# Gates of two branches by Strassen's seven products in a one-core fp32 layer pair

## The reference, cut to what matters

```python
h = rms_norm_2(x, norm_g)
proj = h @ w_in
...
ys = jnp.stack([y_a, y_b, y_c, y_d], axis=0)
branch_d = jnp.einsum('nbsw,nwd->bsnd', ys, w_branch)
g = jax.nn.sigmoid(gates.reshape(bsz, s, N_BRANCH, d))
merged = jnp.sum(g * branch_d, axis=2)
return x + merged @ w_out
```

## Time and profile before

| | us |
|---|---|
| median of 3 runs | 1284.22 (1284.12 to 1284.44) |
| the profiled execution | 1284.06 |
| its span | 1282.3 |
| PE busy in the span | 1274.5 (99%) |
| DVE busy | 718.6 (56%) |
| ACT busy | 567.7 (44%) |
| POOL busy | 32.9 (3%) |

### The profile page before, as it was taken

The page is one execution under the profiler, slowest core; times in us unless marked ns, Lnnn a source line. Parts: engine busy times, 40 slices in busy tenths (PEclk is TensorE's granted clock), DMA queues, the critical chain, the costliest instruction groups (busy, mean ns, idle before and its releaser), DMA issues.

```text
span 1282.3 us, 16218 instructions
## 1 busy us (share of the span) xinstructions
PE 1274.5 (99%) x6041; PEld 1050.8 (82%) x6041; DVE 718.6 (56%) x1497; ACT 567.7 (44%) x1192; POOL 32.9 (3%) x71
## 2 busy tenths in 40 slices
PE   9999999999999999999999999999999999999998
PEld 8888777898888888888888888888878788888887
DVE  5367775754555545448574677764545524444454
ACT  5367665543453344334543323652344532322323
POOL 1000000100000000001100000000000000000000
PEclk9999999999999999999999999999999999999999
DMA  6243442126452646322522322122211222232231
GB/s 248 99 148 108 132 124 83 67 99 199 130 164 74 206 115 197 114 92 92 197 80 99 132 99 99 33 92 106 99 66 66 74 90 100 99 115 96 90 143 66
DMA packets 27038, 145.31 MB, mean 113 GB/s; under 512 B 3400, under 2 KB 3660, under 8 KB 12240
## 3 DMA queue, kind: packets, MB, share of 16 engines
q1 hardware_dynamic: 22920, 130.71, 28.8%
q0 software_dynamic: 1152, 8.39, 3.4%
q10 hardware_dynamic: 2888, 5.18, 1.3%
HBM read 135.87 MB, written 4.20 MB: 109 GB/s over the span
## 4 chain that ended last, share of the span: by engine, by line
PE 96%; DVE 1%; issue 1%; DMA 0%; ACT 0%; POOL 0%; SPq 0%; ACTq 0%; POOLq 0%; DVEq 0%
PE bank L1844 28%; PE bank L1846 27%; PE bank L1845 27%; PE sc L2012 3%; PE tp L2021 2%; PE ob L2078 1%; PE ob L2036 1%; PE bank L1946 1%; PE bank L1956 1%; PE bank L1963 1%; PE sc L1845 1%; PE sc L1846 1%; PE sc L1844 1%; DMA w_raw<-in_weights 0%; POOL rstd L593 0%
## 5 line engine op out<-in xcount | busy, mean ns | idle before, releaser
L1844 PE MATMUL bank<-xT_hi,w_hi 128*128 128x512 f32 (+1 forms) x1136 | 447.7, 394 | 0.1
L1846 PE MATMUL bank<-xT_hi,w_lo 128*128 128x512 f32 (+1 forms) x1136 | 436.4, 384 | 0.0
L1845 PE MATMUL bank<-xT_lo,w_hi 128*128 128x512 f32 (+1 forms) x1136 | 435.9, 384 | 0.0
L1152 DVE TENSOR_TENSOR w_lo<-w_raw,w_hi 128x512 fp32r<-128x512 f32 x412 | 262.4, 686 | 206.8 <-ACT w_hi L659 205.4
L659 ACT ACTIVATE w_hi<-w_raw 128x512 fp32r<-128x512 f32 x412 | 231.1, 621 | 83.6 <-PE bank L1846 80.4
L1844 PEld LDWEIGHTS bank<-xT_hi,w_hi 128*128 128x128 f32 x1136 | 213.7, 188 | 44.6 <-issue 4.5
L1846 PEld LDWEIGHTS bank<-xT_hi,w_lo 128*128 128x128 f32 x1136 | 213.4, 188 | 42.8
L1845 PEld LDWEIGHTS bank<-xT_lo,w_hi 128*128 128x128 f32 x1136 | 213.9, 188 | 39.8 <-issue 1.2
L667 ACT ACTIVATE arena<-bank 128x512 f32<-128x512 f32 x90 | 53.3, 597 | 200.7 <-PE bank L1846 195.6
L1844 PE MATMUL bank<-w_hi,act_hi 128*128 128x512 f32 (+1 forms) x264 | 102.7, 389 | 0.0
L1846 PE MATMUL bank<-w_hi,act_lo 128*128 128x512 f32 (+1 forms) x264 | 101.2, 383 | 0.0
(11 more groups left out here) (230 smaller groups left out, 1418.2 us busy)
## 6 DMA issues: line engine op xcount, KB each, us to landing
w_raw<-in_weights SPq DMA_DIRECT2D x101, 1024.0 KB, 4.8
arena<-in_weights POOLq DMA_DIRECT2D x8, 1024.0 KB, 9.5
arena<-in_weights SPq DMA_DIRECT2D x5, 1024.0 KB, 8.3
arena<-in_bias ACTq DMA_DIRECT2D x16, 256.0 KB, 2.9
act_lo<-act_lo SPq DMA_DIRECT2D x24, 128.0 KB, 2.8
x_sb<-in_x SPq DMA_DIRECT2D x4, 512.0 KB, 6.3
w_raw<-in_weights SPq DMA_DIRECT2D x4, 512.0 KB, 7.8
x_dram<-x_sb SPq DMA_DIRECT2D x1, 2048.0 KB, 11.8
```

What stands on the lines that cost most here:

```text
L1152: nc.vector.tensor_tensor(w_lo[SPLIT_AT[b]][:, cols], w_raw[SLOT[b]][:, cols], w_hi[SPLIT_AT[b]][:, cols].bitcast(F32), ALU.subtract).then ...
L1844: nc.tensor.matmul(ps, hi_l, hi_r, start=first, stop=False, skip_group_check=onto)
L1845: nc.tensor.matmul(ps, hi_l, lo_r, start=False, stop=False, skip_group_check=onto)
L1846: return nc.tensor.matmul(ps, lo_l, hi_r, start=False, stop=last, skip_group_check=onto)
```

## The change

The gates of "c" and "b" (`gate_quad`) are computed with h and the gate's weights cut in 2 x 2 blocks, features x tokens and features x features, by Strassen's seven products (Winograd's form). Each of the seven has 512 output features, 256 tokens and a depth of 512: in chunks, 2 halves x 2 chunks x 4 blocks x 3 products of 256 columns. Here output features lie on partitions.
- Weights: four blocks of 512 x 512 are loaded per branch, two of them a second time or into the extra places; G_SUM_1 to G_SUM_4 are made there by four accumulating transfers from POOL. Seven blocks are split instead of four. An accumulation for G_SUM_2 or G_SUM_4 waits for the split of the sum before it, since it adds onto the same place.
- x forms t1 to t4 (sums and differences of blocks of h, 128 x 1024 each) are made once and serve both branches. DVE makes a raw form from x_hi and x_lo, ACT rounds it, DVE subtracts for the low part. t1 is made in the gates of "d", behind DVE's `split(b + 1)` and ahead of the last four multiply-adds; t2, t3, t4 in "c", behind the splits of G_SUM_1, G_12 and G_SUM_2.
- Products go to `sc0/sc1`, `tp/ob` and `bank2/bank3` in pairs (`GATE_BANK`); ACT copies them out (the third, G_12, with the sigmoid), DVE adds them up in `sig_quad`, ACT applies the sigmoid to the three other quarters. `sig_quad` lies over the raw forms, so ACT waits for all four low parts before its first copy there.
- The multiply-adds then write over `sig_quad`.

The diff, cut to its core:

```diff
+GATE_QUADS = {"c": QUADS, "b": QUADS + 1}
+G_11, G_SUM_1, G_12, G_SUM_2, G_SUM_3, G_22, G_SUM_4 = range(7)
+GATE_BANK = (0, 2, 0, 1, 1, 1, 2)
+GATE_X = ("x11", "t1", "x21", "t2", "t3", "t4", "x22")
...
+        gate_bank = [[sc[0], sc[1]], [tp, ob], [bank[2], bank[3]]]
...
+            def load_gate_quad(f):
+                b = FIRST[f"quad{f}"]
+                load(b + G_11)
+                if f == QUADS:
+                    sp.wait_ge(pv_done, N_UNITS)
+                else:
+                    sp.wait_ge(w_split, PARTS * (FIRST[f"quad{f - 1}"] + G_SUM_4 + 1))
+                sp.dma_start(w_raw[2], stream[STREAM_AT[b, "21"], :, :]).then_inc(w_loaded[2], 16)
+                sp.dma_start(w_raw[3], stream[STREAM_AT[b, "11"], :, :]).then_inc(w_loaded[3], 16)
+                load(b + G_12)
+                load(b + G_22)
...
+            for f in GATE_QUADS.values():   # on POOL
+                b = FIRST[f"quad{f}"]
+                pool.wait_ge(w_loaded[2], 16 * LOADS[b, "21"])
+                add_gate_weights(2, b + G_22, w_chained)
+                pool.wait_ge(w_loaded[3], 16 * LOADS[b, "11"])
+                add_gate_weights(3, (b, "21"), w_paired)
+                pool.wait_ge(w_chained, 16 * (3 * f + 1))
+                pool.wait_ge(w_split, PARTS * (b + G_SUM_1 + 1))
+                add_gate_weights(2, b + G_11, w_chained)
+                pool.wait_ge(w_chained, 16 * (3 * f + 2))
+                pool.wait_ge(w_split, PARTS * (b + G_SUM_2 + 1))
+                add_gate_weights(2, b + G_12, w_chained)
...
+                split(b + G_SUM_1)              # ACT's gate_quad
+                act.wait_ge(gate_add, KD * (r - 1))
+                if f == QUADS:
+                    round_form(1)
+                split(b + G_12)
+                copy_out(G_11, lambda h: p1_of_gate[:, h, :].rearrange("p (m s) -> p m s", s=ST))
+                if f == QUADS:
+                    round_form(2)
+                split(b + G_SUM_2)
+                copy_out(G_SUM_1, lambda h: p5_of_gate[:, h, :].rearrange("p (m s) -> p m s", s=ST))
+                if f == QUADS:
+                    round_form(3)
+                    act.wait_ge(form_split, len(FORMS))
+                split(b + G_SUM_3)
+                copy_out(G_12, quarter(0, 0))
+                copy_out(G_SUM_2, quarter(0, 1))
+                split(b + G_22)
+                copy_out(G_SUM_3, quarter(4, 1))
+                split(b + G_SUM_4)
+                copy_out(G_22, quarter(4, 0))
...
                     split(b + 1)                # DVE's gates
+                    if (br, half) == ("d", 1):
+                        form("t1")
+                        split_form("t1")
                     for c in range(4):
...
+                plus, minus = {"t1": ("x11", "x12"), "t2": ("t1", "x22"), "t3": ("x22", "x12"), "t4": ("t2", "x21")}[n]
+                if plus in form_raw:
+                    combine(form_raw[plus], x_part[minus][0], (ALU.mult, ALU.subtract))
+                else:
+                    combine(x_part[plus][0], x_part[minus][0], ALU.subtract)
+                    combine(raw, x_part[plus][1], ALU.add)
+                combine(raw, x_part[minus][1], ALU.subtract, True)
...
+                split(b + G_SUM_1)              # DVE's gate_quad
+                if f == QUADS:
+                    form("t2")
+                    split_form("t2")
+                split(b + G_12)
+                if f == QUADS:
+                    form("t3")
+                    split_form("t3")
+                split(b + G_SUM_2)
+                if f == QUADS:
+                    form("t4")
+                    split_form("t4")
+                split(b + G_SUM_3)
+                split(b + G_22)
+                fold(0, 1, p1_of_gate, G_11, G_SUM_2)
+                fold(4, 1, p1_of_gate, G_SUM_3)
+                split(b + G_SUM_4)
+                fold(4, 1, p5_of_gate, G_SUM_1)
+                fold(4, 0, p1_of_gate, G_22)
+                split(b + len(LHS))
...
+                for i, name in enumerate(GATE_X):   # PE's gate_quad
+                    where, o = GATE_BANK[i], b + i
+                    if name in FORMS:
+                        pe.wait_ge(form_split, FORMS.index(name) + 1)
+                    for h in range(2):
...
+                        pe.wait_ge(quad_free[where][h], quad_drained(f, i) - 1)
+                        for m in range(2):
+                            for k in range(KW):
+                                if h == 0 and m == 0:
+                                    pe.wait_ge(w_split, PARTS * o + k + 1)
+                                at = W * k + P * (2 * h + m)
+                                last = product(gate_bank[where][h][:, ST * m:ST * m + ST], w_hi[SPLIT_AT[o]][:, at:at + P], w_lo[SPLIT_AT[o]][:, at:at + P],
+                                               x_hi[name][:, k, :], x_lo[name][:, k, :], opens and m == 0 and k == 0, k == KW - 1, True)
```

More of the change, by code:

```diff
@@ L137, in plan @@
     for br in ORDER:
+        if br in GATE_QUADS:
+            f = GATE_QUADS[br]
+            first[f"quad{f}"] = n
+            done += [("quad_full", 2 * (len(LHS) * f + i + 1)) for i in range(len(LHS))]
+            n += len(LHS)
         for half in range(2):
-            add(f"gate_{br}{half}", 2, 4)
+            if br not in GATE_QUADS:
+                add(f"gate_{br}{half}", 2, 4)
             add(f"branch_{br}{half}", 1, 4)
@@ L157, in places @@
     quads = {FIRST[f"quad{f}"]: f for f in range(QUADS)}
+    gate_quads = {FIRST[f"quad{f}"]: f for f in GATE_QUADS.values()}
     def loaded(b, where, place=None):
@@ L173, in places @@
             slot[b + SUM_1], slot[b + SUM_2], slot[b + SUM_3], slot[b + SUM_4] = 2, 2, 3, 2
+            b += len(LHS)
+        elif b in gate_quads:
+            loaded(b + G_11, ordinary % RING)
+            loaded((b, "21"), 2)
+            loaded(b + G_12, (ordinary + 1) % RING)
+            loaded(b + G_22, ordinary % RING)
+            loaded((b, "11"), 3, at[b + G_11])
+            slot[b + G_SUM_1], slot[b + G_SUM_2], slot[b + G_SUM_3], slot[b + G_SUM_4] = 2, 2, 3, 2
+            ordinary += 3
             b += len(LHS)
@@ L428, in quad_drained @@
         def quad_drained(f, i):
-            where = QUAD_BANK[i]
-            return QUAD_BANK.count(where) * f + QUAD_BANK[:i + 1].count(where)
+            order = QUAD_BANK if f < QUADS else GATE_BANK
+            return QUAD_BANK.count(order[i]) * f + order[:i + 1].count(order[i])
         def lhs_at(f, pair_, name):
@@ L649, in split_parts @@
                         if b - FIRST[f"quad{f}"] == SUM_3:
+                            act.wait_ge(w_paired, 16 * (f + 1))
+                    for f in GATE_QUADS.values():
+                        if b - FIRST[f"quad{f}"] in (G_SUM_1, G_SUM_2, G_SUM_4):
+                            act.wait_ge(w_chained, 16 * (3 * f + 1 + (G_SUM_1, G_SUM_2, G_SUM_4).index(b - FIRST[f"quad{f}"])))
+                        if b - FIRST[f"quad{f}"] == G_SUM_3:
                             act.wait_ge(w_paired, 16 * (f + 1))
@@ L1109, in gates @@
                             nc.scalar.activation(mT_hi[:, j, :], merged[:, j, :], ACT.Copy).then_inc(merged_rounded, 1)
+                    if half == 0:
+                        split(b + len(LHS) + 2)
             dsa = attention(U_DSA, N_UNITS, dsa_out)
@@ L1771, in gates @@
                             nc.vector.tensor_tensor(merged[:, j, :], merged[:, j, :], tmp[:, c % 2, :], ALU.add).then_inc(gate_add, 1)
[L1772 to L1775, removed]
+            x_part = {f"x{k + 1}{t + 1}": [part[:, KW * k:KW * k + KW, ST * t:ST * t + ST].bitcast(F32) for part in (xT_hi, xT_lo)]
+                      for k in range(2) for t in range(2)}
@@ L1853, in open_bank @@
                         pe.wait_ge(quad_free[e % 4 // 2][e % 2], quad_drained(f, len(LHS) - 1 if e % 4 >= 2 else PLAIN_21))
+                for br, f in GATE_QUADS.items():
+                    if 0 <= e - USE[f"branch_{br}0"] < 4 and e % 4 >= 2:
+                        pe.wait_ge(quad_free[2][e % 2], quad_drained(f, G_SUM_4))
             def feature_chunk(b, e, c, kc, rhs_hi, rhs_lo, tok=slice(0, S), full=True, steps=None, at=(), arriving=False):
@@ L2278, in _ @@
             for br in ORDER:
-                gates(br)
+                if br in GATE_QUADS:
+                    gate_quad(br)
+                else:
+                    gates(br)
             def merged_ready(i, t, ks):
@@ L2364, in weight_stream @@
         n = BRANCH[br]
+        if br in GATE_QUADS:
+            for kh, fh in ((0, 0), (0, 1), (1, 0), (1, 1)):
+                at = col["gates"][0] + D * n + W * fh
+                blocks.append(pack_rows(w_in, np.arange(W * kh, W * kh + W), r((at, at + W))))
         for half in range(2):
-            for i in range(2):
+            for i in range(0 if br in GATE_QUADS else 2):
                 at = col["gates"][0] + D * n + W * half + 256 * i
```

133 lines of the change are left out of this document (126 added, 7 removed).

## The result

| | us | |
|---|---|---|
| kernel before, run beside it | 1284.17 | 1284.07 to 1284.55, 6 runs |
| kernel after | 1289.72 | 1288.51 to 1290.24, 6 runs |
| ratio | 1.0041 | 95% interval 1.0028 to 1.0054 |
| its profiled execution | 1288.69 | span 1286.9 |

A forecast was written before the change was run, and what follows sets the result against it. TensorE, busy 99% of the span, was taken to bound the kernel. 1284.06 - 6.4 saved on products + 10.4 delay of the fifth product = 1288.1; with the median 0.16 above the profiled execution, 1288.2 us, range 1283 to 1292.5.

The forecast's parts named there:

- the likeliest case: Fifth product of "c" 10.4 us late behind DVE and ACT, nothing late afterwards: 1288.2, own range 1287.3 to 1289.5; chance 0.50.
- rival 1: In "c", the granted clock falls at TensorE's stall before the fifth product: 2.5 us more, 1290.7; chance 0.20.
- Products at 0.120: In both gates, 336 products of 256 columns at 0.120 take 40.32 us, saving 3.20 per branch, 6.40 in all.
- Durations: For the x forms, 1024-element DVE operations take 1.22 us (1.28 from above), ACT's rounding 1.06.
- DVE's list: Ordered DVE work from the end of G_11's split to t4's landing at 1131.6: 36.45 us.
- The chain of ACT behind it: In "c" after t4, ACT splits G_SUM_3, copies out G_12 and G_SUM_2's first half: 3.8 us, to 1135.4.
- How the delay shows: In "c", TensorE waits some 10 us before the second to fifth products, the last behind ACT's copy, others behind DVE's splits.
- Only ordered, not too much: By busy time DVE's work fits in "c" (28 us in 65); by its strict order it doesn't.
- Rival 2: The forms are hidden: with DVE's list done some 10 us earlier, TensorE never waits, 1277.8; chance 0.13.
- Sums in time: Accumulating transfers end before ACT needs them; in "b" G_SUM_2 is there at T + 12.6 and needed at 17.28.
- Rival 3: In "b", the accumulation for G_SUM_2 takes 14.0, TensorE waits some 3 us: 1291.2; chance 0.06.
- The clock: Half rate for part of a product after the stall in "c": 0 to 5.8 us, 2.5 taken; chance 0.20.

The follow-up runs named there:

- second repetition: The kernel after, unchanged, run again on the chip of the run with 24 extra products, for direct comparison: 1289.96 us (1289.54 to 1291.54).
- the faster order: Kernel after with y of "b", t1, t2 made in gaps during "d", raw t3, t4 one step earlier, ACT's wait later: 1278.01 us, 0.9953 to kernel before.
- "b" alone: Against the kernel before, only the gates of "b" by seven products, "c" as before, t1 made in "c", t2 to t4 in "b": 1290.57 us, ratio 1.0049.
- the first step of the order: Kernel after with only y of "b" and t1 moved ahead into DVE's gap during "d": 1285.14 us, ratio 1.0009.
- the filled kernel: Kernel after with 24 extra 256-column products, result unused, before the fifth product of "c": 1288.68 us, against 1289.96 unchanged.
- first repetition: The kernel after, run once more unchanged for a second profile: 1290.01 us (1288.48 to 1291.37).

## Why the prediction held
The time is 1.5 above the forecast and in the stated range. It is not in the likeliest case's own range, 1287.3 to 1289.5: 1289.72 lies between that case (1288.2) and rival 1 (1290.7), and nearer to the rival. So the path was right, and in most executions rival 1's fall came on top of it. The profiled execution, without that fall, is the pure case: 1284.06 + 10.54 of delay + 0.27 of later start - 6.17 saved (3.14 in "b", 3.03 in "c" beside the delay) = 1288.70, and it took 1288.69. By the steps:
- *Products at 0.120.* Right: "b" takes 62.14, predicted 62.1.
- *Durations.* Right: 1.22 to 1.23 for an operation of 1024 elements, as taken from the slope of two narrower rows; 1.06 for ACT's rounding, as taken from its 1024-wide row. The upper bound of 1.28 did not come true.
- *DVE's list.* Predicted 36.45 from the split of G_11 to the last low part; measured from 1095.40 to 1132.26, 36.9. The chain of ACT behind it: predicted 3.8, measured 3.7. The fifth product: predicted 10.4 late, measured 10.54.
- *How the delay shows.* Only in part right. Some 10 us of waits were predicted before the second to the fifth product, the last one 3.7. The delay is there, but the listed waits are 5.6 in all: before the second and the fourth 1.65 and 1.82, before the third none, before the fifth 2.11. The rest was lost while TensorE followed the splits quarter by quarter and ran at the lower clock. In the second repetition, where the fourth product ran at the full clock, the wait before the fifth is 3.61.
- *Only ordered, not too much.* Right, and shown twice: without the forms 1278.97, and with all of them in another order 1278.01. Rival 2 named that time, 1277.8, for forms that are hidden; it was wrong for this order and right for the other.
- *Sums in time.* Right in "b": DVE's split of G_SUM_1 ends at 1179.33 and ACT begins on G_SUM_2 at 1187.89, T + 12.65, where T + 12.6 was computed. Rival 3 did not occur. But the room in "c" was there only since all else was late: without forms that transfer is the next limit (0.8), and rival 2 had no term for it.
- *The clock.* The step that was off. It stood as a rival with 2.5 us and 0.20, as if it happened either always or never. It falls in some executions, at 1.2 to 1.6 each: three of the four profiled executions of this order (the kernel after three times, and the one with ACT's wait moved) had it, and so had the two profiles with a shorter list ("b" alone, and the first step of the order). Of the 16 executions of the kernel after, three took 1288.5 to 1288.7, where the sum lies, and thirteen 1289.5 to 1291.5. So the fall fits most of what the median has above the sum; that it is the rule was not counted, and that the time stayed in the range is owed in part to its price, 1.2 to 1.6 where the rival had put 2.5.

The Trainium skill, "TensorE: Matmul & The Clock Gate", Part 1 (The HAM clock gate), says that the windows run free of the kernel, so that the same kernel measures different amounts of cold work at its start from run to run. The runs agree in kind, in the middle of a kernel: one kernel, the same start of the fifth product, clock 1.00 in one execution and 0.50 in the next.

The start-up is the other part, and no step of the prediction had it: "c" begins 0.27 later than in the kernel before in the execution of the section on the result, 1.26 in the one of the filled kernel. Where the two differ, ACT waits longer for the first weights; why that transfer lands later stays open. The nine executions of the kernel before, run beside the filled one, lie within 0.2 us (1283.93 to 1284.13), so it doesn't show there, and neither does it in the five of the faster order (within 0.3), whose start-up code is the same as that of the kernel after. One execution without the forms (1281.35, 2.4 above its median), in whose profile no wait is left that a fall could follow, was not profiled and stays unexplained. How often start-up and fall come was not counted: only profiled executions tell them apart.

## What to carry to other kernels
An engine that is busy half the time can still set the end, if its list is strictly ordered and each step in it waits for another engine's answer: add the list up row by row from its last free point to the product that needs it, not its busy share. Such a list gets shorter in two ways: move whole items ahead into gaps of the same engine, and where a chain goes producer, other engine, producer, put independent work of the first engine in the middle. Here both together, with one wait of ACT moved, turned +5.5 us into -6.0; the first way alone, on two items, gave 5.1 of delay back, and the second was not tried alone. A last wait of 2.1 to 3.6 us on TensorE came with a lower clock right before or behind its end in five of six profiled executions, and that cost some 1.5 us beyond itself, so price such a fall as likely and not as a yes or no.

## What the runs showed of the hardware
- The granted clock also falls after waits much shorter than the prediction had in mind. In the first execution of the kernel after, the waits before the second and the fourth product are 1.65 and 1.82 us, and both are followed by one; some 3.4 us are run at 1.2 GHz each time (0.43 of the clock is missing over the 4 us of the second row, and a low us misses half: 3.4):
```profile
1112.00:1116.00 4.00, 4.00 (x27) 4.00 (x27) 2.71 (x3) 1.83 (x3) 0.84 (x1) 0.71 0.59 88
...
1128.00:1132.00 4.00, 4.00 (x23) 4.00 (x23) 2.77 (x3) 1.06 (x1) 0.84 (x1) 0.57 0.68 98
```
The prediction had left these shorter waits out of its rival. The first repetition has no fall behind the second product's wait, and the second none behind the fourth's, with the same waits of 1.6 and 1.8. Their fifth product starts just as long after the stage (33.58 and 33.56), so these falls cost nothing: TensorE had to wait for DVE's list again behind them.
- A fall costs less than half of its time: a 256-wide product takes 0.213 in place of 0.120, so 3.4 us at the lower clock do the work of 1.9 and lose 1.5. That is what "c" lost where no slack was behind the fall (74.28 against 72.79).
- The accumulating transfer of 1 MB, from the end of the split that frees its place to ACT's start on the sum: 8.5 in the faster order, 8.6 in "b", 9.4 without the forms. In the first feed-forward quad it was 8.5.
